# Routing of a mixture of experts in a hybrid backbone step: one-hot rows to ScalarE, token weights behind the first expert block, gate rows' difference to GpSimd

## The reference

```python
h = rmsnorm(x, g2) * (1.0 + sc2) + sh2
scores = sigmoid(h @ w_router)                  # 16 experts in 4 groups
sel = scores + b_router
best = argmax over groups of (sum of the top 2 of sel in the group)
idx = top 2 of sel within the best group
w_sel = scores[idx] / sum(scores[idx])
combine = one_hot(idx, 16) * w_sel, summed over the two
a = silu(h @ w_eg[e]) * (h @ w_eu[e]) * combine[e]     # D_EXPERT = 256
x = x + ga2 * sum over e of (a @ w_ed[e])
y = rmsnorm(x, final_g)
```

## Time and profile before

| | |
|---|---|
| median of three runs | 993.54 us |
| profiled execution, its own time | 999.29 us |
| its span, first to last instruction | 997.5 us |
| busy PE, DVE, ACT, POOL | 962.7, 705.1, 440.9, 212.1 us |
| mean granted TensorE clock | 0.985 |
| routing of the last tiles and first tables | 664 to 688 us of the span |
| first expert blocks | 686 us on |

### The profile page before, as it was taken

One profiled execution on the slowest core, in us unless ns is written; L12 is line 12 of the kernel. 1 busy time (PEld: TensorE's weight loads), 2 busy tenths in 40 slices (PEclk: granted clock), 3 DMA queues, 4 the chain that ended last, 5 costly groups with the idle time before them and its releaser, 6 DMA issues.

```text
span 997.5 us, 17439 instructions
## 1 busy us (share of the span) xinstructions
PE 962.7 (97%) x5610; PEld 766.1 (77%) x5611; DVE 705.1 (71%) x1145; ACT 440.9 (44%) x808; POOL 212.1 (21%) x240
## 2 busy tenths in 40 slices
PE   8989999999999999999979999987999999999997
PEld 4889998998999898799956677665677676767675
DVE  4444988155799943369945655778988878787888
ACT  4543211354311135679842333223555555554634
POOL 3020000000000001214441011002353443535423
PEclk7999999999999999999989999999999999999999
DMA  9954344223543313142355333557779999999758
GB/s 360 379 197 148 121 154 178 101 85 107 169 138 118 129 43 97 43 138 65 83 157 195 115 127 133 185 182 235 262 215 284 298 272 315 308 283 284 205 133 331
DMA packets 66399, 183.78 MB, mean 184 GB/s; under 512 B 9602, under 2 KB 22788, under 8 KB 66332
## 3 DMA queue, kind: packets, MB, share of 16 engines
q1 hardware_dynamic: 57060, 150.11, 43.2%
q0 software_dynamic: 7632, 27.79, 11.5%
q10 hardware_dynamic: 1648, 5.10, 1.3%
HBM read 148.81 MB, written 34.16 MB: 183 GB/s over the span
## 4 chain that ended last, share of the span: by engine, by line
PE 84%; DVE 6%; DMA 5%; issue 2%; ACT 1%; SPq 1%; DVEq 0%; POOL 0%; POOLq 0%; ACTq 0%
PE psum L1568 46%; PE psum L1433 23%; PE psum L1551 6%; PE psum L1846 2%; DMA RW<-in_w_in 2%; PE psum L1517 1%; DMA RW<-gm_scratch 1%; DMA RA<-in_w_ada 1%; PE psum L1395 1%; PE psum L1426 1%; DMA RC<-in_w_out 1%; DMA RB<-in_w_exp 1%; PE psum L1737 1%; PE psum L1452 1%; PE psum L1685 1%
## 5 line engine op out<-in xcount | busy, mean ns | idle before, releaser
L1433 PEld LDWEIGHTS psum<-input_parts,weight_parts 128*128 128x128 f32 x1728 | 255.2, 189 | 17.4 <-issue 12.1
L1433 PE MATMUL psum<-input_parts,weight_parts 128*128 128x320 f32 x1728 | 261.8, 312 | 3.8 <-DVE weight_parts L2023 3.8
L1568 PE MATMUL psum<-expert_parts,row_of_slot 128*128 128x512 f32 x404 | 133.7, 396 | 0.6 <-ACT row_of_slot L1309 0.6
L1034 ACT ACTIVATE weight_parts<-RW 128x1024 fp32r<-128x1024 f32 x44 | 46.5, 1058 | 197.0 <-PE psum L1433 150.8
L2023 DVE TENSOR_TENSOR weight_parts<-RW,weight_parts 128x1024 fp32r<-128x1024 f32 x44 | 53.8, 1222 | 101.8 <-ACT weight_parts L1034 101.7
L1568 PE MATMUL psum<-RB,RW 128*128 x216 | 97.8, 595 | 3.7 <-issue 1.6
L1568 PEld LDWEIGHTS psum<-expert_parts,row_of_slot 128*128 128x128 f32 x404 | 75.6, 188 | 23.4 <-issue 7.8
L837 POOL TENSOR_TENSOR RE<-RE,RA 2x2048 f32<-2x2048 f32 x2 | 9.0, 4520 | 326.5 <-DMA RA<-in_b_ada 326.5
L1317 ACT ACTIVATE expert_parts<-RB 128x2048 fp32r x27 | 51.8, 1917 | 52.2 <-DVEq L2550 20.3
L1568 PEld LDWEIGHTS psum<-RB,RW 128*128 128x128 f32 x216 | 38.9, 190 | 43.7 <-issue 43.6
L1568 PE MATMUL psum<-expert_parts,heads_weight 128*128 128x512 f32 x164 | 67.4, 452 | 0.0
(11 more groups left out here) (420 smaller groups left out, 1758.1 us busy)
## 6 DMA issues: line engine op xcount, KB each, us to landing
RB<-in_w_exp SPq DMA_DIRECT2D x96, 512.0 KB, 7.7
RW<-in_w_in SPq DMA_DIRECT2D x44, 512.0 KB, 3.5
RW<-in_w_late SPq DMA_DIRECT2D x32, 512.0 KB, 4.7
RA<-in_w_ada SPq DMA_DIRECT2D x10, 512.0 KB, 12.2
RW<-gm_scratch SPq DMA_DIRECT2D x20, 256.0 KB, 3.4
h_scratch<-RE SPq DMA_DIRECT2D x10, 512.0 KB, 2.6
acc_scratch<-RA SPq DMA_DIRECT2D x10, 512.0 KB, 3.8
RB<-acc_scratch SPq DMA_DIRECT2D x10, 512.0 KB, 8.5
```

Source lines behind the costliest of these rows:

```text
L1034: nc.scalar.activation(spl[:, r, 0], raw[:, r], ACT.Copy).then_inc(whi_ok, 1)
L1433: last = nc.tensor.matmul(psum[:, 2 * r + g, 0:GW], spl[:, r, wv, k], hT[:, xv, k, g * GW:(g + 1) * GW], start=(k == 0 and wv == 0 and xv ...
L1568: return nc.tensor.matmul(out, lhsT, rhs, start=start, stop=stop, **kw_)
```

## The change

- The last tile's squares are taken in two halves on ScalarE, each with its own sum; `root` adds both.
- The token weights leave the routing: their multiplication goes behind the first `x_low`, the four other operations to the head of `slot_weights`. The first `x_low` goes ahead of the first `gate_low`, `slot_rows` behind the first `down_low`.
- The place one-hot rows of the last three tiles are made by ScalarE: (place - column) squared for each of six, then Relu(1 - square) over all. TensorE's `per_slot` waits for them.
- VectorE writes the indices of the first two gathers itself; GpSimd's two copies go.
- The difference of the two gate rows is formed by GpSimd behind the first gather.
- On VectorE the register load of the loop's trip count goes right ahead of the loop; on GpSimd it goes ahead of one refill. In `gate_high(1)` on ScalarE the wait for the token weights comes behind the register loads.
- FILL goes from (0, 36, 48, 52) to (0, 36, 36, 48).

```diff
 def root(n, col):                                     # GpSimd
+    if n == 2 * NT: tensor_scalar(ss1, ss0, ss3, EPS, ALU.add, ALU.add)
+    else:
     tensor_scalar(ss1, ss0, 1.0 / D, EPS, ALU.mult, ALU.add)
...
-        gp.wait_ge(route_ok, 2)
         for b in range(2):
             gp.wait_ge(h2_out[b], STORED)
+        gp.wait_ge(idx_ok, 2)
         for r in range(2):
-            nc.gpsimd.tensor_copy(idxc[:, r], idxU[:, r:r + 1]).then_inc(idx_ok, 1)
-        for r in range(2):
-            gp.wait_ge(idx_ok, r + 1)
             fetch(r)
+        gp.wait_ge(route_ok, 2)
         gp.wait_ge(xg_full[0], 16)
         nc.gpsimd.tensor_copy(idxc[:, 0], idxU[:, 2:3]).then_inc(idx_ok, 1)
...
+        gp.wait_ge(rows_b, 16 * 6)
+        nc.gpsimd.tensor_tensor(ga2[:, 0], ga2[:, 0], ga2[:, 1], ALU.subtract).then_inc(gdiff_ok, 1)
         for j in range(2):
             refill(0, j)
+        gp.wait_ge(route_ok, 4)
+        pairs = gp.value_load(tripm[0:1, 1:2], min_val=1, max_val=NBLK // 2 - 3)
+        refill(1, 0)
         gp.wait_ge(route_ok, 6)
         nc.gpsimd.tensor_copy(idxsc[:, 0], idxS[:, 0:1]).then_inc(idxs_ok, 1)
-        pairs = gp.value_load(...)
-        for j in range(2):
-            refill(1, j)
-            add_rows(j, j, slice(j + 1, j + 2))
+        add_rows(0, 0, slice(1, 2))
+        refill(1, 1)
+        add_rows(1, 1, slice(2, 3))
...
         for t in range(NT):                           # ScalarE, last tile only
+            activation(xr[..HALF[0]], x1[..HALF[0]], ACT.Square, scale=D ** -0.5, accum_out=ss0)
+            h2_transposed(t, (0,))
+            act.wait_ge(x1_ok, X1_ALL)
+            activation(xr[..HALF[1]], x1[..HALF[1]], ACT.Square, scale=D ** -0.5, accum_out=ss3).then_inc(ss_ok, 1)
...
+        act.wait_ge(onehot, 3)
+        for q in range(2 * (NT - BATCH)):
+            c = 2 * BATCH + q
+            ins = nc.scalar.activation(far_slot[:, q], iota, ACT.Square, scale=-1.0, bias=offs[:, c:c + 1])
+        ins.then_inc(sig_ok, 1)
+        act.wait_ge(sig_ok, 3)
+        nc.scalar.activation(offhot_late, far_slot, ACT.Relu, scale=-1.0, bias=1.0).then_inc(sig_ok, 1)
...
         warm(FILL[2], 3)                              # TensorE
-        per_slot(blkhot, 2, 2, 3)
+        pe.wait_ge(sig_ok, 4)
+        per_slot(blkhot, 2, 2, 4)
...
-        then(tensor_tensor(both, hot12, score, ALU.mult))       # VectorE, routing
-        then(tensor_reduce(wtok, both, AX.X, ALU.add))
-        then(tensor_tensor(wsum, wtok0, wtok1, ALU.add))
-        then(reciprocal(wsum, wsum))
-        then(tensor_tensor(wtok, wtok, wsum, ALU.mult))
...
+        nc.vector.scalar_tensor_tensor(idxc[:, :, 0], psum[:, 2, NBLK:NBLK + 2], float(P), blk0[:, 0:2], ALU.mult, ALU.add).then_inc(idx_ok, 2)
         nc.vector.memset(idxU[:, NBLK:NBLK + 1], 0).then_inc(route_ok, 1)
...
-        gate_low(0, slice(0, 1), SPLIT0 + 1)
         x_low(0, 1)
+        token_weights()
+        gate_low(0, slice(0, 1), SPLIT0 + 1)
         slot_weights()
-        slot_rows()
         x_low(1, 2)
         product(0, 1)
         down_low(0, slice(0, 1), SPLIT0 + 2)
+        slot_rows()
         slot_weights_in()
         gate_low(1, slice(1, 2), SPLIT0 + 4)
-        gate_difference()
+        dve.wait_ge(gdiff_ok, 1)
```

More of the change, by code:

```diff
@@ L48 @@
 LAG = 2
-FILL = (0, 36, 48, 52)
+FILL = (0, 36, 36, 48)
 NBMIN = 2 * T // P + 1
@@ L328, in program @@
     idx_ok = sem("idx_ok")
+    gdiff_ok = sem("gdiff_ok")
     xg_full = [sem("xg_full0"), sem("xg_full1")]
@@ L1276, in _ @@
         for t in range(NT):
-            if t == NT - 1:
-                h2_transposed(t, (0,))
-            act.wait_ge(x1_ok, 2 * (t + 1) if t < NT - 1 else X1_ALL)
+            act.wait_ge(x1_ok, 2 * (t + 1))
             if t >= 2:
                 act.wait_ge(h2_out[t % 2], 32 * (t // 2))
-            junk = h2[:, t % 2] if t < NT - 1 else xr[:, t % NX]
-            nc.scalar.activation(junk, x1[:, t % 2], ACT.Square, accum_out=ss[:, 0, t:t + 1]).then_inc(ss_ok, 1)
+            if t < NT - 1:
+                nc.scalar.activation(h2[:, t % 2], x1[:, t % 2], ACT.Square, accum_out=ss[:, 0, t:t + 1]).then_inc(ss_ok, 1)
+            else:
+                nc.scalar.activation(xr[:, t % NX, HALF[0]], x1[:, t % 2, HALF[0]], ACT.Square, scale=D ** -0.5, accum_out=ss[:, 0, t:t + 1])
+                h2_transposed(t, (0,))
+                act.wait_ge(x1_ok, X1_ALL)
+                nc.scalar.activation(xr[:, t % NX, HALF[1]], x1[:, t % 2, HALF[1]], ACT.Square, scale=D ** -0.5, accum_out=ss[:, 3, t:t + 1])\
+                    .then_inc(ss_ok, 1)
             if t == BATCH:
@@ L1309, in a_high, with gate_high @@
             nc.scalar.activation(aTh[:, r].rearrange("p j t -> p (j t)"), psum[:, 6, 0:2 * P], ACT.Copy).then_inc(ah_ok, 1)
-        def gate_high(r, blk, read):
+        def gate_high(r, blk, read, weights=None):
             need = act.value_load(eidI[0:1, blk], min_val=16 * WPART, max_val=16 * WPART * NE)
@@ L1314, in gate_high @@
             act.wait_ge(w_full, need)
+            if weights is not None:
+                act.wait_ge(tok_ps, weights)
             if read is not None:
@@ L1342, in _ @@
         gate_silu(0, 1)
-        act.wait_ge(tok_ps, 2)
-        gate_high(1, slice(1, 2), None)
+        gate_high(1, slice(1, 2), None, 2)
         with act.Fori(0, pairs) as i:
@@ L1903, in _ @@
         pairs = pe.value_load(trip[0:1, 0:1], min_val=1, max_val=NBLK // 2 - 1)
-        per_slot(blkw, 3, 3, 4)
+        per_slot(blkw, 3, 3, 5)
         with pe.Fori(0, pairs) as i:
@@ L2392, in slots_in @@
             then(nc.vector.tensor_reduce(full_of[:, q], passed[:, 0:n], AX.X, ALU.add))
-            then(nc.vector.scalar_tensor_tensor(offs[:, q], full_of[:, q], -float(P), place_in[:, q], ALU.mult, ALU.add))
+            ins = nc.vector.scalar_tensor_tensor(offs[:, q], full_of[:, q], -float(P), place_in[:, q], ALU.mult, ALU.add)
+            if hot is None:
+                ins.then_inc(onehot, 1)
+                return
+            then(ins)
             then(nc.vector.tensor_tensor(hot, offs[:, q].unsqueeze(2).broadcast_to([P, n, P]), iota.unsqueeze(1).broadcast_to([P, n, P]),
@@ L2566, in _, with token_weights @@
         nc.vector.nop().then_inc(route_ok, 1)
+        def token_weights():
+            then(nc.vector.tensor_tensor(both, hot12, te(score).unsqueeze(2).broadcast_to([P, NT, 2, NE]), ALU.mult))
         def slot_weights():
+            then(nc.vector.tensor_reduce(wtok[:, :, :], both, AX.X, ALU.add))
+            then(nc.vector.tensor_tensor(wsum, wtok[:, :, 0], wtok[:, :, 1], ALU.add))
+            then(nc.vector.reciprocal(wsum, wsum))
+            then(nc.vector.tensor_tensor(wtok[:, :, :], wtok[:, :, :], wsum.unsqueeze(2).broadcast_to([P, NT, 2]), ALU.mult))
             w20 = wtok[:, :, :].rearrange("p t j -> p (t j)")
@@ L2644, in _ @@
             dve.wait_ge(h2_out[b], STORED)
+        x_low(0, 1)
+        token_weights()
         gate_low(0, slice(0, 1), SPLIT0 + 1)
-        x_low(0, 1)
         slot_weights()
-        slot_rows()
         x_low(1, 2)
@@ L2661, in _ @@
             gate_low(j, slice(2 + j, 3 + j), SPLIT0 + 7 + 3 * j)
+        pairs = dve.value_load(tripm[0:1, 1:2], min_val=1, max_val=NBLK // 2 - 3)
         with dve.Fori(0, pairs) as i:
```

21 lines of the change are left out of this document (7 added, 14 removed).

## The result

The changed kernel took 997.35 us in the median of 13 runs (993.39 to 1001.83), the kernel before 994.28 in 13 runs alongside. The ratio is 1.0033, 95% interval 1.0017 to 1.0048: **slower by 3.3 us, between 1.7 and 4.8**. The forecast was 0.9 us slower, within what can't be told from no change.

A forecast was written before the change was run, and what follows sets the result against it. The end of VectorE's second gate_low, which TensorE's block 1 split products wait for, was taken as the bound. Terms -0.28 - 0.77 - 0.56 + 0.21 + 1.72 - 1.06 + 1.6 gave +0.9 us: 994.4 from 993.54, range 991.0 to 997.3.

The forecast's parts named there:

- My sign of being wrong: No long VectorE operation beside GpSimd's difference, or block 1's split products on TensorE starting before 703 or after 706.5.
- Squares in two halves: Last tile's sum of squares on ScalarE comes sooner, gain limited by TensorE's logits: -0.28 us, bounds 0 and 0.5.
- Token weights out of the routing: Five VectorE operations leave the routing; the next still needs TensorE's positions, so -0.77 us, bounds 0.6 and 0.9.
- one-hot rows on ScalarE: Ahead of TensorE's per_slot, ScalarE makes the last three tiles' rows and is the later engine: -0.56 us, bounds -0.97 and 0.
- Row numbers by VectorE: In the routing, one more VectorE operation writes the first two gathers' indices: +0.21 us, bounds 0.15 and 0.3.
- The stall, +1.6: GpSimd's difference holds up VectorE's two-operand operations late in the routing: +1.6 us, between 0 and 2.4.
- From the last table to the split products, +0.66: Stretch from routing's end to block 1's split products: token weights add 1.72 us, moving the pairs load saves 1.06.
- The moved token weights: Added on VectorE between the routing and the second gate_low, paid in full there: +1.72 us.
- moving `pairs`: Register load leaves VectorE's idle time ahead of the first gate_low: -1.06 us, bounds 0 and -1.3.
- The rival in which the clock falls: TensorE's clock halves for block 1's split products and what follows: +2.4 us on top of +0.9, 996.8 us; chance 0.10.
- The upper bound of my sum: All terms from the last tile to block 1's split products at their unfavourable ends: +3.8 us; lower bound -1.6.
- the last rival: More comes in than counted: larger start gain, ScalarE keeps pace, no stall: -1.6 us, about 990.4 with run spread; chance 0.07.

The follow-up runs named there:

- the second profile: Changed kernel profiled once more, nothing altered; stretch from last tile's scaling to block 1's split products 46.66 us, against 46.62 in the first.
- e2: Kernel before with only the gate rows' difference moved to GpSimd behind the first gather; ratio to before 1.0027 (1.0014 to 1.0039).
- e3: Changed kernel with the difference back on VectorE behind the second gate_low and the token weights back in the routing; ratio to before 1.0005.
- e7: Changed kernel, GpSimd multiplying one gate row by 1 instead; VectorE forms the difference behind the second gate_low; ratio to before 1.0015.
- e8: Changed kernel with GpSimd's difference in eight pieces of 128 columns instead of one of 1024; ratio to before 1.0008 (0.9989 to 1.0026).
- e4: Changed kernel with 16 small unread products on TensorE behind block 0's second transposes, in its wait for gate_low(0); ratio to before 1.0020.
- e6: e3 with 48 instead of 36 fill products on TensorE ahead of the first per_slot; ratio to before 0.9999 (0.9979 to 1.0020).
- e9: e6 with 12 fill products ahead of block 0's raw-weight group and 52 instead of 48 behind the first per_slot; ratio to before 0.9985.

## Why the prediction was wrong

The bound and the mechanism were right, the sizes weren't. The second `gate_low` set the end before and after (TensorE's wait of 1.52 us ahead of 699.25), and GpSimd's difference came out as the largest term. The sum gave +0.86 and the stretch +3.08. Of the 2.22 us between them, 0.87 came behind the last table, where the register loads were mis-sized, 0.60 is the stall, 0.19 the row numbers and 0.64 the first piece, up to the logits; the last is not in the second profile. My sign of being wrong, block 1's split products after 706.5, came true: laid on the clock of before by the anchors they start at 707.33. The terms one by one:

- *Squares in two halves*, -0.28: the sum of squares did come earlier, but VectorE then waited 0.56 us for the logits, for which TensorE's clock had fallen to 0.50 some 2 us earlier against the anchor than before. +0.36 in the first profile, -0.17 in the second. The excess is the clock's, not the change's: e2, whose code is that of before up to here, has 4.13 where before has 3.66. Where the clock fell no earlier than before (the second profile, e3) or not here at all (e7, e8), the changed code took 3.48 or 3.49, so the term itself is about -0.17.
- *Token weights out of the routing* -0.77, measured -0.76; *one-hot rows on ScalarE* -0.56, measured -0.64. No table was loaded for the Relu. The Trainium skill (ScalarE: Activation LUTs, Table sets: the hidden batching unit) has relu in every set, and the trace agrees.
- *Row numbers by VectorE* +0.21: +0.40, of which 0.23 is L2553, 0.41 us where it took 0.18. It ended 0.01 us ahead of GpSimd's DMA_INDIRECT for the gather (672.36 to 673.60); in all ten profiles with the new index write it took 0.40 or 0.41 and ended 0.01 or 0.02 ahead of that instruction. Before, the same operation started 0.65 us into the DMA_INDIRECT instead of 0.82 and took 0.18 (L2533 at 682.15). So a hold by the last part of that instruction would fit, but no run tests it. Dropping GpSimd's two copies, for which I took 0.8, brought the gather nothing: it starts 0.93 us behind the end of VectorE's index write, before 0.97. It came 1.3 us later than forecast (680.44 on the clock of before, not 679.1), 0.64 of it by the late logits, and GpSimd's difference behind it 1.2 later.
- **The stall, +1.6: the first mis-sized term.** It was 2.20 us. I had GpSimd's duration right (2.4, measured 2.35) but took off for VectorE operations that would run beside it. It began in the worst place, where L2579 was about to start; that was chance. e2 shows that counting on one-operand operations was wrong as well: a tensor_scalar with one SBUF operand waited 1.58 us there. Of those seen, only the reduction ran at its usual speed. The Trainium skill (Advanced Engine Details and Errata, VectorE Performance Modes) says that GpSimd's instructions block, and are blocked by, VectorE's instructions in a mode that uses two ports, and its table gives tensor_scalar such a mode, but not tensor_tensor and tensor_reduce. The trace agrees for the tensor_scalar in e2 and for the reduction; it shows a tensor_tensor with two SBUF operands held too (L2579). The hold lasted until GpSimd's instruction ended (2.35 us, 1.04 in e7), and with short instructions until the short one ended (e8).
- **From the last table to the split products, +0.66: the second mis-sized term.** It was +1.53. The moved token weights cost their 1.72 as forecast. The register load for which I took 0.8 us, so that moving `pairs` would win 1.06, takes 1.06 behind a waited-for result, and 0.26 came ahead of `x_low`, so only 0.57 was won. And 0.34 more came at `down_low`, whose register load is queued behind the wait for silu; silu was late by the half clock in block 0's split products. In e4, where the clock stayed up, these 0.34 us are gone.

The rival in which the clock falls was half right: the clock did fall, but in block 0's split products and not in block 1's, and there it cost 0.4 to 0.6 us, not 2.4 (e4), because TensorE had the slack. The upper bound of my sum, 3.8 us, held the measured difference, and yet the time lies 0.05 us above the range. That it is outside is the base's doing: the forecast stood on the median of three runs, 993.54, and the median of 13 is 994.28, 0.74 higher. The sum was off without that: +0.9 where 3.3 were measured. Two slips in the working changed nothing: 1.89 - 0.8 is 1.09, not 1.06, and the last rival's terms give 990.1, not 990.4. What is left open is why the clock falls where it does: it moved by several microseconds between kernels that were the same up to that point.

## What to carry to other kernels

Before work is given to GpSimd because it is free there, look at what VectorE does at that moment: if it is a serial chain on the critical path, one long GpSimd instruction can cost VectorE nearly its full length (2.20 of 2.35 us here, 1.58 of 2.56 in e2). Cut such work into short instructions, or leave it on VectorE behind the point that sets the end: there its 1.22 us gave TensorE no wait up to block 2's products. Moving operations along a chain of one engine only helps if they go past the point where that chain is waited for. The moved token weights stayed ahead of it, and at their old place 0.98 of their 1.7 us had been hidden in a wait for TensorE.

## What the runs showed of the hardware

- A held VectorE operation ends behind GpSimd's by its own usual duration less 0.13 to 0.15 us: as if it did its work when the other is done. L2579 (0.42) ended 0.29 us behind, in e7 0.27, L2564 in e2 (0.17) 0.03, and L2240 before (0.68) 0.55. A tensor_reduce of 256 columns beside GpSimd took its usual 0.42 (e2, e8). In e2 a VectorE operation that started 0.07 us ahead of GpSimd's wasn't held, and GpSimd's took 0.21 longer.
- GpSimd's instruction with one operand (e7) held VectorE up like those with two.
- A register load on VectorE cost 1.06 us behind a result that is waited for, and 0.36 where an instruction without a wait stood ahead of it (e3).
- A fall of TensorE's clock cost 0.4 to 0.6 us where VectorE set the end (e4), and made a 1.38 us wait on VectorE (0.35 without it) where TensorE's chain was close behind (e6 and e9).
